# Streaming a constant matrix through TensorE in the first eleven steps of an attention

## What is computed

```python
h = rms_norm(x, norm_mix[l])
z = h @ w_in[l]                       # queries, keys, values, recurrence, convolution
q_a, k_a = rope(rms_norm(q_a)), rope(rms_norm(k_a))
o_att = block_attention(q_a, k_a, v_a)           # 8 heads of 64, 2 key heads, full softmax
o_hg = hgrn2_bidirectional(...)                  # gated recurrence, 4 heads of 64
o_cv = conformer_conv(a_c, g_c, conv_w[l], ...)  # 31 taps, layer norm, silu
x = x + concatenate([o_att, o_hg, o_cv]) @ w_out[l]
h = rms_norm(x, norm_mlp[l])
x = x + square(relu(h @ w_mlp_in[l])) @ w_mlp_out[l]
```

## Time and profile before

| | |
|---|---|
| three executions | 3772.72, 3774.63 and 3774.76 us, median 3774.63 |
| the profiled execution | span of 3772.8 us from first to last instruction; the profile gives no other time of it |
| mean granted clock of TensorE | 0.980 |
| busy: TensorE, its weight loads | 97%, 74% |
| busy: VectorE, ScalarE, GpSimd | 57%, 35%, 32% |
| attention of layer 0, first scores to the last slot with additions | about 221 to 277 us |
| attention of layer 1, the same | about 901 to 957 us |

### The profile page before, as it was taken

How to read it: one execution, slowest core, us unless ns; L and a number is a source line. 1 busy time by engine, 2 the same in 40 slices (tenths; PEclk the granted TensorE clock), 3 DMA queues, 4 the chain that set the end, 5 groups by cost and what they waited for, 6 DMA issues and landing times.

```text
span 3772.8 us, 44713 instructions
## 1 busy us (share of the span) xinstructions
PE 3647.3 (97%) x17876; PEld 2805.4 (74%) x17876; DVE 2131.7 (57%) x3000; ACT 1336.3 (35%) x2282; POOL 1195.8 (32%) x486
## 2 busy tenths in 40 slices
PE   8989999998999999999999999999999999999998
PEld 6646888865688878577777678887767777778887
DVE  7887565788655564633363585456553255365444
ACT  6354121534521132545333432122344433342212
POOL 0003444200244443132323244444213232334443
PEclk9989999998999999999999999999999999999999
DMA  4101333220133342021222133234112221223332
GB/s 139 40 12 62 97 99 95 90 63 12 45 95 95 97 140 81 29 79 56 78 62 73 56 91 99 95 95 148 46 45 73 62 79 62 65 73 94 99 95 84
DMA packets 80798, 292.39 MB, mean 77 GB/s; under 512 B 9648, under 2 KB 11088, under 8 KB 80080
## 3 DMA queue, kind: packets, MB, share of 16 engines
q1 hardware_dynamic: 77808, 278.49, 23.5%
q10 hardware_dynamic: 2784, 11.03, 0.9%
HBM read 285.30 MB, written 2.10 MB: 76 GB/s over the span
## 4 chain that ended last, share of the span: by engine, by line
PE 86%; DVE 9%; issue 2%; ACT 2%; DMA 0%; SPq 0%; DVEq 0%; ACTq 0%
PE acc L336 24%; PE acc L338 23%; PE acc L337 23%; PE banks L607 2%; PE banks L656 2%; PE banks L977 2%; PE banks L639 2%; PE banks L994 1%; PE banks L1731 1%; DVE stat L743 1%; DVE QK L892 1%; DVE conv_c L1396 1%; DVE near L920 1%; DVE pair L408 1%; PE banks L614 1%
## 5 line engine op out<-in xcount | busy, mean ns | idle before, releaser
L280 POOL TENSOR_TENSOR w_lo<-w_raw,w_hi 128x1024 fp32r<-128x1024 f32 x482 | 1195.6, 2481 | 2549.9 <-ACT w_hi L233 2549.9
L233 ACT ACTIVATE w_hi<-w_raw 128x1024 fp32r<-128x1024 f32 x518 | 549.0, 1060 | 1717.3 <-PE acc L338 1638.1
L336 PE MATMUL acc<-hH,w_hi 128*128 128x512 f32 x1776 | 729.7, 411 | 11.8 <-DVE sig L2119 6.6
L338 PE MATMUL acc<-hL,w_hi 128*128 128x512 f32 x1776 | 698.6, 393 | 0.0
L337 PE MATMUL acc<-hH,w_lo 128*128 128x512 f32 x1776 | 697.8, 393 | 0.0
L336 PEld LDWEIGHTS acc<-hH,w_hi 128*128 128x128 f32 x1776 | 337.3, 190 | 97.8 <-issue 25.7
L336 PE MATMUL acc<-H,w_hi 128*128 128x512 f32 x1024 | 400.5, 391 | 3.8 <-DVE L L400 3.8
L336 PE MATMUL acc<-midH,w_hi 128*128 128x512 f32 x1024 | 401.0, 392 | 0.3
L371 DVE TENSOR_TENSOR xT<-acc,xT 128x512 f32<-128x512 f32 x160 | 110.6, 692 | 511.3 <-PE acc L338 498.9
L337 PE MATMUL acc<-midH,w_lo 128*128 128x512 f32 x1024 | 398.7, 389 | 0.0
L338 PE MATMUL acc<-midL,w_hi 128*128 128x512 f32 x1024 | 398.6, 389 | 0.0
(11 more groups left out here) (338 smaller groups left out, 4720.3 us busy)
## 6 DMA issues: line engine op xcount, KB each, us to landing
w_raw<-in_stream SPq DMA_DIRECT2D x518, 512.0 KB, 3.6
cw<-in_cmpw ACTq DMA_DIRECT2D x2, 2048.0 KB, 7.5
mixed<-in_cmpw ACTq DMA_DIRECT2D x2, 2048.0 KB, 12.9
x_tok<-in_x SPq DMA_DIRECT2D x2, 1024.0 KB, 7.6
out<-probsT SPq DMA_DIRECT2D x4, 512.0 KB, 4.0
stack<-Z ACTq DMA_DIRECT2D x8, 128.0 KB, 2.3
stack<-Z ACTq DMA_DIRECT2D x8, 127.8 KB, 2.4
masks_f<-in_masks SPq DMA_DIRECT2D x1, 960.0 KB, 12.1
```

The source lines that it names most:

```text
L233: act.activation(w_hi[:, u % WB, 0:w], w_raw[:, u % 2, 0:w], ACT.Copy).then_inc(hi_split, 1)
L280: pool.tensor_tensor(w_lo[:, u % WB, 0:w], w_raw[:, u % 2, 0:w], w_hi[:, u % WB, 0:w], ALU.subtract)\
L336: pe.matmul(acc[n % 2][:, :], wh, H[:, k, :], start=(k == 0), stop=False)
L338: last = pe.matmul(acc[n % 2][:, :], wh, Lo[:, k, :], start=False, stop=(k == nk - 1))
```

## The change

In slots 0 to 10 of the attention of layers 0 and 1, TensorE now issues three more products at the end of the slot's transposition and before whatever `conv_pe` issued there: the identity in bf16 as the stationary operand, all of `Cb` (128x512) streamed, into acc[1], which nothing reads before slot 13 overwrites it. In slot 0 the first of them waits until the last two tiles of `late_in` have been taken out of acc[0] and acc[1].

```diff
+WARM = 3
...
+                    late_first = FIRST_TILE[layer, "late_in"]
+
                     def conv_pe(slot):
+                        if slot < CONV_NORM:
+                            if slot == 0:
+                                for n in (late_first + 6, late_first + 7):
+                                    pe.wait_ge(acc_free[n % 2], n // 2 + 1)
+                            for _ in range(WARM):
+                                pe.matmul(acc[1][:, :], identb, Cb[:, :, :].rearrange("p i c -> p (i c)"),
+                                          start=True, stop=True)
                         if slot == att.n:
```

## The result

Twenty runs of each kernel: 3775.06 us before (3772.72 to 3776.79), 3780.68 after (3773.54 to 3782.88). The ratio is 1.0014, 95% interval 1.0008 to 1.002: the change costs some 5.6 us, 0.14%. That is within the 0.2% named in the prediction, but 0.2 us above the range and on the slower side. The twenty runs are not spread evenly: one took 3773.54, the other nineteen 3778.4 to 3782.9.

What follows compares the result with a forecast made beforehand. VectorE was taken to bound the changed slots, except where TensorE's value products of slots 6 and 10 are on the path. A layer summed to 0 + 0.69 + (0.69 - 1.38) = 0.00, so 3774.63 us; range 3769.5 to 3780.5.

Steps and rivals of the forecast that it cites:

- What bounds the kernel; slots 0 to 5: Early attention slots: VectorE hardly waits, 0.14 us before slot 2, so additions there were costed at 0.
- Slot 6: Three additions on the path before slot 7's scores: +0.69 us, value product unchanged at 5.35.
- I take 5.35 again: Slot 6's value product stays at 5.35 us, between possible 3.58 and 7.16, as no addition fills the hole ahead.
- the clock is held: Rival, chance 0.30: full clock through slots 1 to 10, both value products 3.58; -1.91 us a layer, 3770.8 in all.
- Slot 10: Additions before slot 11's scores +0.69 us; value product 3.58 instead of 4.96, -1.38, slot 9's additions filling a low stretch.
- The sum of a layer: Slots 0 to 10 of one attention: 0 + 0.69 + (0.69 - 1.38) = 0.00 us; no change, chance 0.42.
- Additions do nothing for the clock: Rival, chance 0.18: clock unaffected in the attentions, +2.53 us a layer, +5.1 in all, 3779.7.
- +1.15: Slot 1, clock still low: three additions delay slot 2's maxima by 1.29 us, less 0.14 of slack.
- the rule that was weighed: Trainium skill's rule that transposes do not bring TensorE to full clock; attention's low stretches would then stay.
- From slot 11 on nothing is added and the chain is the same; a shift passes on one for one: Behind slot 11, any shift reaches the end unaltered, since the stage behind it is TensorE's.
- falls of the clock at other places behind slot 11: Rival, chance 0.03: the clock falls elsewhere after slot 11; thought small, all shifting by a part of a microsecond.

Runs made afterwards that it cites:

- second execution: Later profiled execution of the changed kernel, nothing further altered; it took 3782.92 us, span 3781.6.
- With the hole ahead of it filled: Changed kernel, but slots 6 and 10 have four additions between scores and value product; 3773.0 against 3775.08 before; with six more in slot 15, 3773.01 against 3775.24.
- the kernel with two products in both layers: Changed kernel plus two such products ahead of the first down projection in layers 0 and 1; 3780.14 us against 3775.08 for the kernel before.
- first execution: Earlier profiled execution of the changed kernel, nothing further altered; it took 3778.4 us, span 3777.1.
- the trace with five products: Kernel before, attentions unchanged, plus five such products ahead of layer 1's first down projection; 3779.31 us, +5.2 us over the kernel before.
- four products in both layers: Changed kernel plus four such products ahead of the first down projection in layers 0 and 1; 3778.01 us against 3775.24 for the kernel before.
- four in layer 0: Changed kernel plus four such products ahead of layer 0's first down projection alone; 3774.40 us against 3774.95 for the kernel before.
- eleven: Kernel before, attentions unchanged, plus eleven such products ahead of layer 1's first down projection; 3778.1 us, +4.0 us over the kernel before.
- fourteen in another layer: Kernel before, attentions unchanged, plus fourteen such products ahead of layer 0's first down projection; 3782.78 us against 3775.08 before.
- the repeated changed kernel: Changed kernel measured again as it is, beside the kernel before; 3781.87 us against 3774.12, ratio 1.0015.

## Why the prediction was wrong

*What bounds the kernel; slots 0 to 5.* Right in both executions. In the second the maxima of slot 2 start 9.55 us after the first score (232.63 - 223.08), before 9.78 (231.24 - 221.46): -0.23, where the prediction took 0 and named 0.14 as all there was to win. VectorE bounds the stretch: with a clock of 0.67 instead of 0.50 that quarter of a microsecond is all.

*Slot 6.* Right on the additions: +0.65 for +0.69. Its value product is again 5.35 in two of the four attentions of the two traces, but 6.55 and 6.58 in the others, which "I take 5.35 again" did not allow for: +1.2 us each. With the hole ahead of it filled it is 3.65 in all four attentions traced. But 3.65 comes without that too: in layer 0 of the kernel with two products in both layers, whose attention is that of the change, both value products read

```profile
251.11 3.65 PE banks L661 x16
...
271.54 3.65 PE banks L661 x16
```

and this attention is 1.99 us shorter than before, where the case "the clock is held" had -1.91. So that case did come, in a single attention.

*Slot 10.* The number is right: +0.65, and -1.31 for -1.38. The sum of a layer is -0.23 + 0.65 + 0.65 - 1.31 = -0.24; the attentions with the same alignment give -0.26 to -0.31. Forecast: 0.00. The reason given, that the three of slot 9 fall into the low stretch ahead, isn't shown: with additions in slots 6 and 10 alone the product of slot 10 takes as little, in layer 0

```profile
271.13 3.65 PE banks L657 x16
```

*Additions do nothing for the clock.* Its time, 3779.7, came within a microsecond of the median, for none of its reasons: no layer has its +1.15, and the clock is 0.67 there. That is luck; a time that fits says nothing of its mechanism. Whether transpositions alone bring the clock up, the rule that was weighed, no run here decides, since the additions are no transpositions.

*"From slot 11 on nothing is added and the chain is the same; a shift passes on one for one."* **This is the step that failed.** In the second execution an attention 0 shorter by 0.26 us was followed by +1.85 at the beginning of layer 1, +2.4 in its attention and +3.2 behind it. The distance from slot 11's maxima to the end, which was to stay unchanged, is 3502.5 us there, before 3495.1. In the first execution it is 3495.9: of its 4.3 us, 3.5 lie ahead of slot 11's maxima, 2.55 of these ahead of the attention. The prediction had the mechanism and gave it 0.03, "falls of the clock at other places behind slot 11", because "all of it shifts by a part of a microsecond"; that smallness was the wrong reason. The rows for a better guess were at hand: the clock's falls inside the attentions cost 1.4 to 1.8 us each at a value product, so one new fall weighs as much as the largest term of the sum. The range had one microsecond for the spread of the runs beyond the cases; the thirty runs of the changed kernel spread over 9.6. (The range is also added up wrongly: 3770.8 and 3779.7 with one microsecond each way are 3769.8 and 3780.7, which would just hold the median of 3780.68, with the mechanism no better.)

*What stays open.* Each row of the tables is one execution. The two of the changed kernel differ in where they lose, and they differ ahead of the attention already: the first scores come between 221.1 and 224.4 us in the traces of all these kernels, though up to there the program is the same. In the five traces with nothing added to the attentions it is 221.1 to 222.6, in the six with all the additions of the change 221.5 to 224.0. Whether that is chance isn't shown, nor therefore how much of the 5.6 us lies ahead of all that changed. The kernel before reaches layer 1 undisturbed in both its traces, even from an attention of 86.54 us, but in the trace with five products the same instructions do not. Why the changed kernel is disturbed so much more often that 26 of its thirty times lie above 3778 us isn't shown. Nor is it by which shift exactly layer 2 goes wrong: it does with four products in both layers and not with four in layer 0.

## What to carry to other kernels

A local sum of a few tenths of a microsecond is not a forecast for the whole when TensorE's clock falls at its waits, as it does here: every later stage with a wait is a place where a shift of either sign can buy or cost a low stretch of some microseconds. Before an addition (or a saving) of that size is judged, delay the stage behind it by a few hundred nanoseconds of idle work, in both kernels; if that moves the time by more than the delay, the verdict is one on alignment. Work that is to hold the clock belongs in the hole ahead of the step that is slow, not behind it: there the value products were at 3.65 us or less in every attention traced, behind it in two of twelve at slot 6. The whole kernel did not get faster by it beyond the intervals.

## What the runs showed of the hardware

The price of a place was not expected: five bf16 products of 0.22 us moved the whole by 5.2 us, eleven by 4.0, fourteen in another layer by 7.7, and four in one layer by -7.5 against the repeated changed kernel (3774.40 to 3781.87, in separate sets of runs). One attention, its instructions unchanged, took 82.05, 83.74 or 86.54 us by where the low stretches lay in it. With the additions, a low stretch that began 7.65 us ahead of the first score went with 86.10 us, one that began 7.71 us ahead of it with 81.75. The Trainium skill (TensorE: Matmul & The Clock Gate, section Part 1) says that the number of products at the low clock, while it comes up, differs from run to run of the same kernel, that this ramp costs under one per cent of a typical kernel's span, and that one should not fit to a particular count. The traces agree: the two of the kernel before have 83.74 and 86.54 us in attention 0, and all of the 8.8 us are 0.23% of this span. But the 8.8 us were also more than everything that the change did locally.

The additions themselves ran at 0.65 us for three at full clock, 0.22 each, where the nearest row had 0.23.
